# One decoder step: the last projection of the sparse-attention layer takes in six turnings of queries and keys, the rotation is cut in parts, ScalarE copies the tokens at the start, and page copies go ahead of a weight split

## The reference, cut to what matters

```
h = rms_norm(x, norm_mix_pre[0]);  z = h @ e_w_in[0]         # layer 0, EVEN_IN = 3072 columns
mix = concat(retention, gating) @ e_w_out[0]                 # layer 0, output projection
kc, vc = compress(gather_pages(cache_cmp, page_table))       # 16 pages of 128 rows, layer 1
z = h @ o_w_in[0]                                            # layer 1: q 1024, k and v 1536, gates 48
q, k = rope(q), rope(k)                                      # first 16 of the 64 values of a head
o_c = softmax(q kc / 8) vc                                   # compressed branch, also selects blocks
o_s, o_w = softmax(q k / 8) v                                # selected and window branch
y = (g0 o_c + g1 o_s + g2 o_w) @ o_w_out[0]
```

## Time and profile before

| what | value |
|---|---|
| median of three runs | 1625.67 us (1625.23 to 1625.72) |
| the profiled execution | 1625.51 us |
| its span | 1623.8 us |
| mean granted clock of TensorE | 0.993 |
| PE busy | 1583.1 us, 97% of the span |
| PEld busy | 1413.8 us, 87% |
| DVE, ACT, POOL busy | 792.7, 678.9, 229.9 us |
| the chain that ended last | PE 92%, DVE 4%, ACT 2% |

### The profile page before, as it was taken

How to read it: one execution, slowest core, us unless ns; L and a number is a source line. 1 busy time by engine, 2 the same in 40 slices (tenths; PEclk the granted TensorE clock), 3 DMA queues, 4 the chain that set the end, 5 groups by cost and what they waited for, 6 DMA issues and landing times.

```text
span 1623.8 us, 30186 instructions
## 1 busy us (share of the span) xinstructions
PE 1583.1 (97%) x12487; PEld 1413.8 (87%) x12487; DVE 792.7 (49%) x1293; ACT 678.9 (42%) x1289; POOL 229.9 (14%) x574
## 2 busy tenths in 40 slices
PE   8999999999999999999999999999999999999998
PEld 7799988699999999997677656667989999999997
DVE  4855452555532555337233576743175552355523
ACT  4222144455532555324322566654355552354522
POOL 3000001300000000002013344432020000000001
PEclk9999999999999999999999999999999999999999
DMA  6322238023233232322343400024202323333231
GB/s 206 123 81 82 89 84 195 13 78 94 71 95 96 79 102 62 95 69 79 112 132 66 177 7 1 1 97 99 78 27 78 98 59 111 88 84 97 58 90 55
DMA packets 180274, 138.38 MB, mean 85 GB/s; under 512 B 11408, under 2 KB 164272, under 8 KB 180112
## 3 DMA queue, kind: packets, MB, share of 16 engines
q1 hardware_dynamic: 172288, 113.26, 24.4%
q0 software_dynamic: 7888, 23.79, 5.1%
HBM read 128.21 MB, written 13.01 MB: 87 GB/s over the span
## 4 chain that ended last, share of the span: by engine, by line
PE 92%; DVE 4%; ACT 2%; issue 1%; POOL 1%; DMA 0%; DVEq 0%; ACTq 0%
PE gemm L1046 42%; PE gemm L676 19%; PE gemm L687 10%; PE misc L645 6%; PE gemm L1185 2%; PE misc L1216 2%; PE misc L794 1%; PE misc L1336 1%; PE misc L698 1%; PE misc L770 1%; PE gemm L756 1%; PE gemm L794 1%; DVE y L1789 1%; PE misc L785 1%; PE gemm L1180 1%
## 5 line engine op out<-in xcount | busy, mean ns | idle before, releaser
L1759 DVE TENSOR_TENSOR wL<-raw,wH 128x2048 fp32r<-128x2048 f32 (+1 forms) x106 | 219.7, 2073 | 192.1 <-ACT wH L1371 191.9
L1046 PE MATMUL gemm<-hH,wH 128*128 128x272 f32 x1280 | 268.6, 291 | 0.1
L1046 PE MATMUL gemm<-hH,wL 128*128 128x272 f32 x1280 | 264.8, 288 | 0.0
L1046 PE MATMUL gemm<-hL,wH 128*128 128x272 f32 x1280 | 264.0, 288 | 0.0
L1371 ACT ACTIVATE wH<-raw 128x2048 fp32r<-128x2048 f32 (+2 forms) x110 | 185.8, 1690 | 83.2 <-PE gemm L676 32.7
L1046 PEld LDWEIGHTS gemm<-hH,wH 128*128 128x128 f32 x1280 | 200.6, 188 | 5.9 <-issue 4.1
L1046 PEld LDWEIGHTS gemm<-hL,wH 128*128 128x128 f32 x1280 | 201.1, 189 | 0.0
L1046 PEld LDWEIGHTS gemm<-hH,wL 128*128 128x128 f32 x1280 | 199.9, 189 | 0.0
L2047 DVE SCALAR_TENSOR_TENSOR conv<-up,rows_t,conv 128x560 f32<-128x560 f32 x88 | 70.6, 802 | 208.9 <-ACT conv L1371 208.9
L1371 ACT ACTIVATE up<-gemm 128x32 f32<-128x32 f32 (+2 forms) x264 | 66.0, 324 | 175.9 <-PE gemm L1046 153.6
L676 PE MATMUL gemm<-hH,wH 128*128 128x272 f32 (+1 forms) x624 | 133.4, 295 | 0.8 <-issue 0.5
(11 more groups left out here) (374 smaller groups left out, 2690.5 us busy)
## 6 DMA issues: line engine op xcount, KB each, us to landing
raw<-in_f_w_in SPq DMA_DIRECT2D x88, 512.0 KB, 5.0
raw<-in_f_w_out SPq DMA_DIRECT2D x32, 704.0 KB, 4.6
raw<-in_e_w_in SPq DMA_DIRECT2D x12, 1024.0 KB, 5.2
raw<-in_o_w_in SPq DMA_DIRECT2D x10, 1024.0 KB, 5.0
raw<-in_e_w_out SPq DMA_DIRECT2D x4, 1024.0 KB, 6.5
raw<-in_o_w_out SPq DMA_DIRECT2D x16, 256.0 KB, 7.4
pages<-in_cache_cmp POOLq DMA_DIRECT2D x10, 256.0 KB, 4.5
xin<-in_x_prompt SPq DMA_DIRECT2D x4, 512.0 KB, 6.2
```

Of the source, the lines that this page charges most:

```text
L1046: ins = pe.matmul(gemm[odd][:, n, 0:TH], w, x[:, k, n * TH:(n + 1) * TH], start=(k == 0 and part == 0), stop=(k == nk - 1 and part == 2))
L1759: order(dve.tensor_tensor(unit_view(wL, u), unit_view(raw, u), unit_view(wH, u).bitcast(F32), ALU.subtract), lo_ready)
```

## The change

Four things, none of which changes what is computed.

**1. The last unit of layer 1's input projection.** The first six turnings (`turn_in(0)` to `turn_in(5)`) move from behind the last unit into it: two behind each of its token tiles 1, 2 and 3. ACT and DVE copy them out behind their copies of the unit's results. The rotation of the last 512 query columns is cut by tiles: 0 and 1, 2 and 3 inside the unit (`turn_tiles`), tile 4 behind the first mask of the attention. ACT's `split_hi(O_OUT)` and its table load move into the unit as well. The `stay_busy` of 8 and of 3 and 3 and 3 and 3 behind the unit are gone. The sample queries are turned in step 7 of the attention, and copied by DVE in step 8; `split_lo(O_OUT)` moves to step 16; the clearing of `qS` goes ahead to unit 9. For that, `qT0` stands in the first four chunks of `hL`, heads and rows of the output weights change places accordingly (1 - j), and the score banks start with `gemm[1]`.

**2. The start.** ACT copies the turned raw tiles 1, 2 and 4, DVE tile 3. The first quarter of `wH` comes ahead of the copy of tile 2. PE turns chunk 0 before the raw tile 4, the sample rows before chunk 1, and enters the first unit with two chunks turned, the others in pairs behind chunks 0, 1 and 2.

**3. The output projection of layer 0.** ACT has `take_pages` ahead of `split_hi`.

**4.** SP waits for the copy of the sample queries before it loads rows into their place.

The diff, cut to its core:

```diff
-        qT0 = sb("qT0", [P, R, SEQ], at=HL_AT + 4 * T * 4)
+        qT0 = sb("qT0", [P, R, SEQ], at=HL_AT)
...
+        def score_slot(n):
+            return gemm[(n + 1) % 2]
...
+            sp.wait_ge(qk_ev[1], 7)
...
+            def turn_in(n):
+                j, z = TURNS[n]
+                bank = 2 + n % 2 if n < 6 else 3
+                if n == 0:
+                    pe.wait_ge(o_ropes, 5)
+                elif (j, z) == (1, 0):
+                    pe.wait_ge(o_ropes, 8)
...
+            def turn_sample_queries():
+                pe.wait_ge(qk_ev[1], 6)
+                for z in range(8):
+                    turn(b7[:, z * NS:(z + 1) * NS], qN[0:NS, 0, z * P:(z + 1) * P], qs_turned if z == 7 else None, k=NS)
...
-                        if u == E_IN and k < 2:
-                            for dc in ((3, 4, 5), (6, 7))[k]:
-                                turn_normal(dc)
+                        if u == E_IN and k < 3:
+                            turn_normal(2 * k + 2)
+                            turn_normal(2 * k + 3)
...
                     if part:
                         order(ins, gemm_done)
+                        if u == O_OUT - 1 and t < 4:
+                            turn_in(2 * t - 2)
+                            turn_in(2 * t - 1)
...
+            pe.wait_ge(x_scaled, NT)
+            turn_normal(0)
+            pe.wait_ge(tile_in[4], 16)
+            pe.wait_ge(x_rooted, NT + 3)
+            turn_tokens(4)
             for dc in range(DC):
                 turn(b4[:, dc * NS:(dc + 1) * NS], xn[0:NS, 0, dc * P:(dc + 1) * P], ...)
-            pe.wait_ge(x_scaled, NT)
-            for dc in range(3):
-                turn_normal(dc)
+            turn_normal(1)
+            pe.wait_ge(xt_ready, 2)
+            pe.wait_ge(x_rooted, NT + 4)
...
-            stay_busy(8)
-            pe.wait_ge(o_ropes, 7)
-            for z in range(8):
-                turn(b4[:, z * NS:(z + 1) * NS], qN[0:NS, 0, z * P:(z + 1) * P], ...)
...
-            for n in range(6):
-                if n >= 2:
-                    stay_busy(3, b5)
-                turn_in(n)
...
                 if 1 <= n < 7:
                     turn_in(5 + n)
+                elif n == 7:
+                    turn_sample_queries()
...
+            take_tokens(1, 2)
+            act.wait_ge(raw_ready[0], landed[0])
+            weight_quarter(0, x_rooted)
+            take_tokens(2, 3)
             act.wait_ge(gain_ready, 1)
             for k in range(DC):
-                act.wait_ge(xt_turned, 8 + k)
+                act.wait_ge(xt_turned, 8 + k if k else 6)
                 activate(hH[:, k, NS:T], misc[:, 1 + k % 3, :], ACT.Copy, h_hi, scale=gains[:, k, 0:1])
+                if k == 0:
+                    take_tokens(4, 7)
+                elif k < 4:
+                    weight_quarter(k, x_rooted if k < 3 else hi_ready)
...
+                            if j == 0:
+                                split_hi(first + i + 1)
...
+                    if n == 10 and j < 3:
+                        take_in(2 * j)
+                        if j == 1:
+                            split_hi(O_OUT)
+                            activate(root_probe[:, :], eps[:, 0:1], ACT.Exp)
...
+                if n == 10:
+                    take_in(1)
+                    turn_tiles(0, 2)
+                    take_in(3)
+                    turn_tiles(2, 4)
+                    take_in(5)
                     continue
...
+                if n == 0:
+                    turn_tiles(4, NT)
                 if 1 <= n < 7 and n % 2 == 0:
                     take_in(5 + n)
+                elif n == 8:
+                    take_sample_queries()
+                elif n == 16:
+                    split_lo(O_OUT)
```

More of the change, by code:

```diff
@@ L1514, in project_out @@
                 for i in range(4):
-                    split_hi(first + i + 1)
-                    if first == O_OUT and i == 0:
-                        load_root()
+                    if first == O_OUT:
+                        split_hi(first + i + 1)
+                        if i == 0:
+                            load_root()
                     for j in range(2):
@@ L1641, in _ @@
                     activate(vcP[:, :, :], b6[0:NCP, 0:2 * P].rearrange("p (j e) -> p j e", j=2), ACT.Copy)
-            split_hi(O_OUT)
             meet(act, order, 3)
@@ L2111, in _ @@
                     order.wait()
-            split_lo(O_OUT)
-            dve.wait_ge(cp_done, 2)
-            order(dve.memset(qS[:, :, :, :, :], 0.0))
-            dve.wait_ge(qs_turned, 1)
-            order.wait()
-            for j in range(2):
-                for g2 in range(2):
-                    half = slice(64 * g2, 64 * g2 + 64)
-                    order(dve.tensor_copy(qS[half, :, j, g2, 0:16].rearrange("p b (r n) -> p r b n", r=R),
-                                          b4[half, j * P:(j + 1) * P].rearrange("p (r b n) -> p r b n", r=R, b=DB)))
             meet(dve, order, 3)
@@ L2445 @@
 PHI_LOADS = 16 * 4
-X_ROOTED, X_SCALED = NT + 3, NT + 3
+X_ROOTED, X_SCALED = NT + 6, NT + 3
 E_LOADS = 16 * 15
```

168 lines of the change are left out of this document (96 added, 72 removed).

## The result

| | median us | all runs |
|---|---|---|
| kernel before | 1625.45 | 1625.06 to 1625.72, 4 runs |
| changed kernel | 1613.36 | 1612.11, 1613.32, 1613.39, 1619.82 |
| ratio | 0.9936 | 95% interval 0.992 to 0.9953 |

The forecast was 1613.2 (1609.0 to 1618.0). Six more runs of the changed kernel lie between 1611.28 and 1619.96; over all ten the median is again 1613.36. This spread of 8.7 us, against 3.7 in 24 later runs of the kernel before (1622.9 to 1626.6), is the second finding, and the profiled execution of the changed kernel (1619.82, span 1618.1) is one of the two slowest.

A forecast was written before the change was run, and what follows sets the result against it. PE, busy 97% of the span, was taken to bound the kernel, so only its idle, filled or lower-clock time could gain. Terms -4.4 - 1.2 - 10.0 + 3.1 = -12.5 gave 1613.2 us, range 1609.0 to 1618.0.

The forecast's parts named there:

- Start: Start of the kernel: first products at 20.1, second unit at 36.4 instead of 40.86, so -4.4 us.
- Pages: Layer 0's output projection: copies ahead of the split, then a 2.3 us PE wait for late page loads; -1.2 us.
- 3 us at chunk 6: Output projection, layer 0: gain from idle 0.7 instead of 2.44 and turnings of 0.87 instead of 1.6.
- Unit to attention: Layer 1's last projection unit to first scores: 13.5 us removed, 2.6 and 0.9 added, scores at 887.2; -10.0 us.
- Attention: Attention loop: sample queries, their copies and the last split moved in delay PE; +3.1 us, ends 0 and 5.4.
- (a): Attention and second unit: the insertions and the wait are covered, 0 instead of +3.1, 1610 us; chance 0.15.
- (b): Idle PE stretches at 35 and 278: the lower clock moves there, up to 1.9 us each, 1617.0; chance 0.17.
- (c): Ahead of the attention: ACT not free once its table is loaded, 0.7 us paid, 1613.9; chance 0.08.
- (d): Last unit's turnings: PE waits for banks, about 1.5 us for each of three groups, 1617.7; chance 0.09.
- (e): Attention's first two groups: PE stays at the lower clock, +24 us, 1637, slower than before; chance 0.03.
- its sign of being wrong: First attention groups: a clock window under 1.00 there would show the forecast wrong.
- with hardly any idle time behind, it stays: Attention, the last split ahead of step 14's reciprocal: 2.29 us late makes PE late by 2.0, not recovered.

The follow-up runs named there:

- after: The profiled execution of the changed kernel, with nothing further changed: 1619.82 us, span 1618.1.
- start_only: The kernel before with only the start's part of the change: median 1621.13 us, ratio 0.998.
- pages_only: The kernel before with only the page copies put ahead of the split in layer 0's output projection: median 1622.59 us, ratio 0.9985.
- attn_only: The kernel before with only the turnings in the last unit, the rotation in parts and what moved into the attention: median 1619.81 us, ratio 0.9972.
- fill_both_waits: The changed kernel with unused PE products filling its waits at attention steps 10 and 18: median 1611.87 us, ratio 0.9917.
- again: The changed kernel run six more times, unchanged: median 1614.84 us, ratio 0.9947; its trace is of a quick run, 1611.28.
- both_in_gaps: The changed kernel with DVE's last split ahead of the attention's first mask and the sample queries' copies at step 12: median 1609.85 us, ratio 0.991.
- gaps_filled: both_in_gaps with two unused PE products ahead of each turning at attention steps 10, 11 and 12: median 1611.69 us, ratio 0.9914.
- split_twice: The changed kernel with DVE's split at attention step 16 done twice, same result: median 1620.08 us, ratio 0.9966.

## Why the prediction was right

- *Start*, -4.4. The first products at 20.27 (forecast 20.1), the second unit at 36.76 (36.4), with ACT's last `hH` beginning at 31.08 and both splits in the chain. Measured by the marks: -4.0 in after, -4.1 in *start_only*. The lower clock did not come back behind the new idle 1.34.
- *Pages*, -1.2. The order and the next thing late were right; the wait was 1.14 instead of 2.3, but a second of 0.92 came for the last pages, which the forecast had not named. *pages_only*: -1.3 by the marks (2.0 less the 0.7 that it was ahead at the second unit). There the wait of 2.3 did not come at all: PE's waits in this stage are 0.64, 0.65, 0.79 and 0.49, against 2.44, 0.65 and 0.69 before, which is 1.2 less. So the term had the right size with a wait in it that no trace shows at that length. The 3 us at chunk 6 are 2.5 by the forecast's own figures (2.44 less 0.7, and 1.6 less 0.87); the term does not use them.
- *Unit to attention*, -10.0. Measured -9.7 in *attn_only* (605.06 less 595.32 from the reciprocal to the first score) and the same in after. The missing 0.3 is that the filling (`stay_busy(4)`) took 1.15 where 0.9 had been set down. ACT was free at 880.14, early enough.
- *Attention*, +3.1. The mechanism was right at both steps, and the wait at 18 was 1.87 where 2.0 was forecast. Without any lower clock the attention of *fill_both_waits* is 2.8 longer than before: 1.9 of it the wait for the split, 0.6 PE's turnings of the sample queries, 0.3 the queries' copies (in *again* PE's waits of steps 8 to 14 are 2.37 together instead of 2.08); the forecast had 2.0 and, for the last two, 1.1. *both_in_gaps* keeps 0.5 (175.45 less 174.92), about the turnings alone, with its waits of steps 8 to 14 back at 2.08. What was missing is the price behind the waits: a stretch of 3.4 costs 1.4 (179.15 less 177.74), the two of 6.8 in after 4.8 together (182.54 less 177.74). This is the term that was mis-sized: +3.1 was +4.2 in two traces and +7.6 in a third.
- *The sum*. With the terms as the marks have them, without the lower clock in the attention, it is -4.1 - 1.3 - 9.7 + 2.8 = -12.3, against -12.5. That the median came out at 1613.4, 0.2 from the forecast, owes something to luck: the attention cost more than forecast, and in *again* the stretch at the lower clock that before and after have near 795 was gone. By the medians of the three parts, the start and the third part gave less and the pages more. The ten runs reach from 1611.3 to 1620.0, three of them above the forecast's 1618.0, which is no range of one forecast but of one kernel.
- *Rivals*. (a) fell: the insertions were paid. (b) came, with another place and price: it put the stretches at 35 and 278, at 1.9 each; they came in the attention, at 1.4. (c) fell: the probe begins at 880.03, 0.01 behind the table load's end, and no further drain as in the Trainium skill's page "ScalarE: Activation LUTs", section "What ACT_TABLE_LOAD costs", is seen here either. (d) fell: the groups of turnings take 0.87 each and the dozens between them 2.75 to 3.00, with no bank waited for. (e) did not come as a whole, yet its sign of being wrong, a window under 1.00 in the first attention groups, did: 0.96.

The step that has to be put differently is "with hardly any idle time behind, it stays". It stays, and it is followed by a slower clock, and this was forecast for idle time elsewhere only.

## What to carry to other kernels

Work that is moved off a chain lands somewhere: look for an idle stretch of its new engine that ends in a wait with room (here DVE's 2.66 ahead of the first mask, where 2.29 cost PE nothing), not for a step at which the engine's average load is low. A PE wait of 1 to 2 us in a stretch of short products can cost about as much again in clock (here 1.4 behind one of 1.87). Removing it and filling it are both worth trying, and filling it tests cheaply whether idle time is the cause. Read from the trace in which step a wait lies before filling it (*gaps_filled* missed by one to two steps). Where two profiles of one kernel differ by more than the change is worth, compare stretches between marks, and look at the granted clock first.

## What the hardware showed that was not expected

- The lower level came behind waits as short as 1.02 us, and once (*split_twice*, 993.9) behind one of 0.73, where the whole attention before had 1.00 with waits of 0.73 and 0.65 in it.
- A table load is followed by the next ACTIVATE within 0.01 us (878.74 plus 1.28 is 880.02; 880.03).
- The same program's runs can agree within 0.5 us in one set (three runs of the kernel before, 1625.23 to 1625.72) and spread over 3.7 in another (24 runs, 1622.90 to 1626.63), with the granted clock between 0.993 and 0.995.
